# An mLSTM layer on Trainium2: decays put on the queries, the finish of its rows moved between its chunk steps

## What is computed

```python
log_d = jnp.where(tri, cum[..., :, None] - cum[..., None, :] + ig[..., None, :], NEG_INF)
inter = cum + m_st[..., None]
m_t = jnp.maximum(inter, jnp.max(log_d, axis=-1))
s_qk = jnp.einsum('bhctd,bhcsd->bhcts', q, k) * jnp.exp(log_d - m_t[..., None])
a_t = jnp.exp(inter - m_t)
num = (jnp.einsum('bhcts,bhcsv->bhctv', s_qk, v)
       + a_t[..., None] * jnp.einsum('bhcvk,bhctk->bhctv', c_st, q))
den = jnp.sum(s_qk, axis=-1) + a_t * jnp.einsum('bhck,bhctk->bhct', n_st, q)
out = num / jnp.maximum(jnp.abs(den), jnp.exp(-m_t))[..., None]
```

## Time and profile before

| | |
|---|---|
| median of 3 executions | 1573.1 us |
| lowest, highest | 1570.92, 1576.23 us |
| profiled execution, its own time | 1573.14 us |
| its span in the profile | 1571.3 us |
| outside the span (1573.14 less 1571.3) | 1.8 us |
| TensorE's granted clock over the span | 0.98 |
| TensorE busy | 1469.6 us, 94% |
| VectorE busy | 995.1 us, 63% |
| ScalarE busy | 755.6 us, 48% |
| GpSimd busy | 67.5 us, 4% |

### The profile page before, as it was taken

How to read it: one execution, slowest core, us unless ns; L and a number is a source line. 1 busy time by engine, 2 the same in 40 slices (tenths; PEclk the granted TensorE clock), 3 DMA queues, 4 the chain that set the end, 5 groups by cost and what they waited for, 6 DMA issues and landing times.

```text
span 1571.3 us, 24144 instructions
## 1 busy us (share of the span) xinstructions
PE 1469.6 (94%) x9392; PEld 1204.5 (77%) x9392; DVE 995.1 (63%) x2286; ACT 755.6 (48%) x1630; POOL 67.5 (4%) x76
## 2 busy tenths in 40 slices
PE   6999998999999999999979999798899899999998
PEld 4777756787777777888757777576687798789987
DVE  4647676564666548535674668576776567777753
ACT  4435576453655443231133546565566447555542
POOL 0000000100000100020000100001100120000000
PEclk9999999999999999999999999899999999999999
DMA  9131172322452322221461153514435542445553
GB/s 360 56 107 54 54 256 81 101 81 67 157 191 69 107 89 92 94 68 54 155 234 54 55 166 104 175 55 141 144 125 159 186 169 95 158 152 189 189 188 132
DMA packets 59866, 202.84 MB, mean 129 GB/s; under 512 B 7694, under 2 KB 10984, under 8 KB 59624
## 3 DMA queue, kind: packets, MB, share of 16 engines
q1 hardware_dynamic: 53568, 192.84, 35.6%
q10 hardware_dynamic: 6008, 7.40, 2.0%
q0 software_dynamic: 176, 1.06, 0.2%
HBM read 199.43 MB, written 1.84 MB: 128 GB/s over the span
## 4 chain that ended last, share of the span: by engine, by line
PE 71%; DVE 15%; ACT 5%; DMA 4%; issue 3%; POOL 1%; ACTq 0%; SPq 0%; DVEq 0%; POOLq 0%
PE ps L2216 65%; PE ps L2219 5%; DVE w_l L2886 2%; DVE st L2985 1%; DMA w_raw<-in_l_out 1%; DVE x L2894 1%; ACT w_h L2529 1%; DVE l_P L2890 1%; ACT l_P L2532 1%; DMA w_l_ada<-in_l_ada 1%; DVE m_P L3469 1%; DVE l_xn L2890 1%; DVE l_h_lat L2894 1%; POOL mstat L3563 1%; POOL pstat L3574 1%
## 5 line engine op out<-in xcount | busy, mean ns | idle before, releaser
L2886 DVE TENSOR_TENSOR w_l<-w_raw,w_h 128x1024 fp32r<-128x1024 f32 (+3 forms) x263 | 315.0, 1206 | 82.5 <-ACT w_h L2529 81.6
L2529 ACT ACTIVATE w_h<-w_raw 128x1024 fp32r<-128x1024 f32 (+3 forms) x263 | 271.1, 1042 | 111.9 <-DMA w_raw<-in_l_out 26.7
L2216 PE MATMUL ps<-w_h,l_hTh 128*128 128x512 f32 (+1 forms) x384 | 156.4, 407 | 0.3 <-DVE w_l L2886 0.2
L2216 PE MATMUL ps<-w_h,l_hTl 128*128 128x512 f32 (+1 forms) x384 | 152.1, 396 | 0.0
L2216 PE MATMUL ps<-w_l,l_hTh 128*128 128x512 f32 (+1 forms) x384 | 151.9, 396 | 0.0
L2532 ACT ACTIVATE l_P<-ps,st 128x512 f32<-128x512 f32 (+1 forms) x128 | 77.5, 606 | 84.7 <-DVE st L2894 59.2
L2216 PE MATMUL ps<-f_hTh,w_h 128*128 128x256 f32 x352 | 99.1, 281 | 0.0
L2216 PE MATMUL ps<-l_hTh,w_h 128*128 128x512 f32 (+1 forms) x264 | 98.5, 373 | 0.5 <-issue 0.5
L2216 PE MATMUL ps<-f_hTl,w_h 128*128 128x256 f32 x352 | 98.9, 281 | 0.0
L2216 PE MATMUL ps<-f_hTh,w_l 128*128 128x256 f32 x352 | 98.8, 281 | 0.0
L2216 PE MATMUL ps<-l_hTl,w_h 128*128 128x512 f32 (+1 forms) x264 | 97.7, 370 | 0.0
(11 more groups left out here) (444 smaller groups left out, 3475.7 us busy)
## 6 DMA issues: line engine op xcount, KB each, us to landing
w_raw<-in_l_ada SPq DMA_DIRECT2D x49, 512.0 KB, 4.6
w_raw<-in_l_z SPq DMA_DIRECT2D x32, 512.0 KB, 3.5
w_raw<-in_l_adg SPq DMA_DIRECT2D x32, 512.0 KB, 3.5
w_raw<-in_l_out SPq DMA_DIRECT2D x32, 512.0 KB, 4.5
w_raw<-in_m_merge SPq DMA_DIRECT2D x24, 512.0 KB, 3.2
w_raw<-in_f_gate SPq DMA_DIRECT2D x22, 512.0 KB, 3.3
w_raw<-in_f_up SPq DMA_DIRECT2D x22, 512.0 KB, 3.5
w_raw<-in_f_down SPq DMA_DIRECT2D x22, 512.0 KB, 4.3
```

The lines of the kernel that those rows point to most:

```text
L2216: return p.e.matmul(out, lhsT, rhs, start=start, stop=stop)
L2529: return p.e.activation(out, a, func, scale=scale)
L2886: return p.e.tensor_tensor(out, a, b, op)
```

## The change

- A query's state part is scaled before the matmul. The row `a` is halved and split in two parts (tiles `l_arl`, `l_arc`), four matmuls spread it over all partitions (`ml_scaled`, `l_ar*,l_pick`), and VectorE multiplies the queries by it (tile `l_qk`, or `l_k` in steps 4 and 5). The state's four matmuls, of 257 columns, then add to the same PSUM group as the local ones. The small matmuls, four operations of the denominator's chain, `ml_carried` and `ml_edge` are gone.
- The finish of a context tile is done tile by tile and sooner, and its transposes start before step 6; `fin_o`, squares and rows of latent tile 1 lie beside step 7.
- The gate row's 8 modulation blocks come first, with `ahead` 1 for 2.
- `split_to` at the end goes to out 3 rather than out 1. The rest of out 1 and out 3 is taken by GpSimd (`POOL_REST`), with a semaphore per slot.

```diff
+POOL_REST = {("l2_out", 1), ("l2_out", 3)}
...
-            weave(beside, upto(half, 8), 8, 14)
+            weave(beside, upto(half, 8), 8, 11)
...
-        mod = p.ada(PAIR, [(3, 0), (2, "gate"), (3, 1)], gate, ahead=2)
-        drain(braid(upto(steps, 6), upto(mod, 6), upto(ctx, 3)))
+        mod = p.ada(PAIR, [(2, "gate"), (3, 0), (3, 1)], gate, ahead=1)
+        weave(braid(upto(steps, 6), upto(mod, 6)), upto(ctx, 7), 7, 12)
         gate.free = p.fence()
-        drain(braid(steps, mod, ctx))
-        p.W.split_to(len(p.W.order) + 1, len(p.W.order) + 1)
+        weave(braid(upto(steps, 3), upto(mod, 3)), upto(ctx, 4), 4, 6)
+        lat = m.finish((1, 0), lambda: f, TRANS)
+        weave(braid(steps, mod), braid(upto(lat, 3), ctx), 6, 6)
+        p.W.split_to(len(p.W.order) + 3, len(p.W.order) + 3)
         f = p.fence()
-        lat = m.finish(LAT, f, TRANS)
...
+        def scaled(x):
+            d, c = steps[x]
+            b = p.take(pool)
+            p.ml_scaled(self, x, d, self.ORDER[d][c], b, self.qa(x))
+            p.give(b, ("lstm", "qa", x))
...
             if x < 6:
+                scaled(x + 2)
                 masked(nxt)
...
         for t in pair:
             p.fin_o(self, t, [self.htok[t, h] for h in range(4)])
             yield
-        for t in pair:
             p.fin_sq(self, t)
+            p.rows_rstd4(self, t)
             yield
-            p.rows_rstd4(self, t)
-        for t in pair:
             p.fin_rows(self, t)
             yield
...
+            y = p.mm(p.n.bank(bo[h], 257), m.Dt[x][:, h * 128:h * 128 + 128], m.va[:, t, h, :], True, c == 0)
+            if c == 0:
+                y.then_inc(*p.mark("lstm", "sum", x, h))
         for h in range(4) if c else ():
-            p.wait_ge(("lstm", "den", x))
-            p.mm(p.n.bank(bo[h])[:, 257:512], m.qk[:, h, t * 128:t * 128 + 128], m.C[:, 4 * d + h, 0:255], True, True).then_inc(
-                *p.mark("lstm", "carry", x, h))
+            p.wait_ge(("lstm", "qa", x), ("lstm", "C", x - 2, h))
+            p.mm(p.n.bank(bo[h], 257), m.qa(x)[:, h], m.C[:, 4 * d + h, :], False, True).then_inc(*p.mark("lstm", "sum", x, h))
+
+    def ml_scaled(p, m, x, d, t, b, out):
+        s0 = slice(t % 2 * 128, t % 2 * 128 + 128)
+        p.wait_ge(("gates", "ar"), p.B.freed[b])
+        for h in range(4):
+            pick = m.pick[:, 4 * d + h:4 * d + h + 1].to_broadcast([128, 128])
+            y = p.mm(p.n.bank(b)[:, h * 128:h * 128 + 128], pick, m.ar[t // 2][:, s0], True, True)
+        y.then_inc(*p.mark("lstm", "spread", x))
...
+    def ml_scaled(p, m, x, d, t, b, out):
+        four = p.n.bank(b).rearrange("p (h t) -> p h t", h=4)
+        p.wait_ge(("lstm", "spread", x), ("lstm", "qk", t), ("lstm", "state", x - 4, 3) if x in (4, 5) else None)
+        p.tt(out, m.qk[:, 0:4, t * 128:t * 128 + 128], four, ALU.mult).then_inc(*p.mark("lstm", "qa", x))
```

More of the change, by code:

```diff
@@ L953, in __init__ @@
         self.rounded = self.done = 0
+        self.rests = [0] * NR
     def next(self, name, i, ks, cols, raw=False, ahead=AHEAD):
@@ L959, in next @@
         b.nsplit = self.split_n
+        s = b.j % NR
         if not raw:
             self.split_n += 1
+            self.rests[s] += 1
+        b.rest, b.on_pool = (s, self.rests[s]), (name, i) in POOL_REST
         self.order.append(b)
-        s = b.j % NR
         view = lambda t: t[:, 0:ks * cols].rearrange("p (k n) -> p k n", k=ks)
         b.raw, b.h, b.l = view(n.w_raw[s]), view(n.w_h[s]), view(n.w_l[s])
-        b.ready = [("loaded", b.j)] if raw else [("w_rounded", b.nsplit), ("w_rest", b.nsplit)]
+        b.ready = [("loaded", b.j)] if raw else [("w_rounded", b.nsplit), ("w_rest", *b.rest)]
         self.p.w_load(b.j + NR)
@@ L1647, in chunks @@
         self.kE = lambda d, c: self.k0[d][:] if c == 0 else self.kt[:, self.ORDER[d][c], :]
+        rows = lambda t: self.qk[:, 0:4, t * 128:t * 128 + 128]
+        self.qa = lambda x: (self.k0[x - 4][:].rearrange("p (h t) -> p h t", h=4) if x in (4, 5) else
+                             rows(self.ORDER[steps[x][0]][steps[x][1]]))
         def exponents(x):
@@ L1671, in chunks @@
             bo = [p.take(pool) for _ in range(4)]
-            p.ml_local_mm(self, x, t, bo)
-            bd = p.take(pool) if c else None
-            p.ml_den(self, x, d, c, t, bo, bd, self.dn_tok.get((d, c - 1)))
-            if c:
-                p.give(bd, ("lstm", "last", x))
-            p.ml_carry_mm(self, x, d, c, t, bo)
-            dtok[x] = ("lstm", "carry" if c else "local", x, 3)
+            p.ml_local_mm(self, x, d, c, t, bo)
+            p.ml_den(self, x, d, t, bo, self.dn_tok.get((d, c - 1)))
+            dtok[x] = ("lstm", "sum", x, 3)
             yield
@@ L2686, in ml_max @@
         p.f(r["a"][:], r["a"][:], ACT.Exp).then_inc(*p.mark("gates", "a"))
+        p.wait_ge(("gates", "a"), p.stage_tok)
+        for x in range(2):
+            y = p.copy(m.ar[x][0:64], r["a"][:, 256 * x:256 * x + 256], scale=0.5)
+        y.then_inc(*p.mark("gates", "ah"))
         p.wait_ge(("gates", "nm_in"))
@@ L3151, in ml_max @@
         p.tt(m.negMr[64:128], m.negM[:], m.negMr[0:64].bitcast(F32), ALU.subtract).then_inc(*p.mark("gates", "M"))
+        p.wait_ge(("gates", "ah"))
+        for x in range(2):
+            y = p.stt(m.ar[x][64:128], r["a"][:, 256 * x:256 * x + 256], 0.5, m.ar[x][0:64].bitcast(F32), ALU.mult, ALU.subtract)
+        y.then_inc(*p.mark("gates", "ar"))
     def ml_cols(p, m, b, fence):
@@ L3200, in ml_masked, with ml_den @@
         p.tt(D[:], D[:], m.ST[:, t, :], ALU.mult).then_inc(*p.mark("lstm", "D", x))
[L3202 to L3205 removed]
+    def ml_scaled(p, m, x, d, t, b, out):
+        four = p.n.bank(b).rearrange("p (h t) -> p h t", h=4)
+        p.wait_ge(("lstm", "spread", x), ("lstm", "qk", t), ("lstm", "state", x - 4, 3) if x in (4, 5) else None)
+        p.tt(out, m.qk[:, 0:4, t * 128:t * 128 + 128], four, ALU.mult).then_inc(*p.mark("lstm", "qa", x))
+    def ml_den(p, m, x, d, t, bo, prev):
+        n, dn = p.n, m.dn[:, d]
+        p.wait_ge(("lstm", "sum", x, 3), prev)
         for h in range(4):
@@ L3219, in ml_den, with ml_local @@
         p.e.reciprocal(dn[:, 1], dn[:, 1]).then_inc(*p.mark("lstm", "recip", x))
-        if c:
-            p.wait_ge(("lstm", "recip", x))
-            p.stt(dn[:, 2], dn[:, 1], 0.5, a, ALU.mult, ALU.mult).then_inc(*p.mark("lstm", "gain", x))
-            p.wait_ge(("lstm", "gain", x))
-            p.tt(dn[:, 3], two[:, :, 0], dn[:, 2], ALU.mult).then_inc(*p.mark("lstm", "last", x))
-    def ml_local(p, m, x, d, c, t, h, b, fresh, old):
+    def ml_local(p, m, x, d, t, h, b, fresh, old):
         dst, src = m.h[t][:, h * 256:h * 256 + 256], p.n.bank(b, 256)
-        p.wait_ge(("lstm", "last" if c else "recip", x), ("lstm", "carry", x, h) if c else None)
+        p.wait_ge(("lstm", "recip", x))
         if fresh:
@@ L3566, in condition, with w_rest @@
         p.e.memset(p.n.phalf[:], -0.5).then_inc(*p.mark("begin", "half"))
+    def w_rest(p, b):
+        n, s, w = p.n, b.j % NR, b.words
+        if b.on_pool:
+            p.wait_ge(("w_rounded", b.nsplit))
+            out, raw, high = n.w_l[s][:, 0:w], n.w_raw[s][:, 0:w], n.w_h[s][:, 0:w].bitcast(F32)
+            p.e.tensor_tensor(out, raw, high, ALU.subtract).then_inc(n.sem(f"w_rest{s}"), 1)
     def rows_mean(p, rows, t):
```

71 lines of the change are left out of this document (21 added, 50 removed).

## The result

The changed kernel is **slower**: 1578.1 us (median of 20, 1573.0 to 1583.1) beside 1572.7 for the kernel before on the same chip, a ratio of 1.0037, 95% interval 1.0026 to 1.0049. Forecast was 1569.2, in a range of 1563.5 to 1574. A second set of executions gave 1.0041 (1.0027 to 1.0055).

What follows compares the result with a forecast made beforehand. TensorE (94% busy) was taken to wait for the late latent rows on VectorE's queue; 1573.1 less 5.3 gives 1567.8, with 2.4 for a GpSimd hold and queued power 1570.2, middle -3.9: 1569.2, range 1563.5 to 1574.

Steps and rivals of the forecast that it cites:

- stage -4.7: Modulation and out stage behind the z projection: the part of the forecast -3.9 beside the z projection's +0.8.
- the forecast's two cases: Whole kernel: 1567.8 us after a gain of 5.3, or 1570.2 with one VectorE hold and the queued power, 2.4.
- Two savings and four spreads fall into the z projection, where TensorE has no gap, +0.8: z projection: saves about 0.8 us per state group, pays 0.6 per spread of four matmuls; net +0.8.
- Rival 4: z projection: scaling doesn't pay; a scaled tile delaying a mask costs 0.7 in each of four steps, +3; no chance given.
- I cost them at nothing: Gates: two added roundings and two operations of 256 columns on VectorE, beside the query and key projection, cost nothing.
- the case that the cover is gone: Gates: if blocks were not split several ahead, the four added VectorE operations would cost 4 x 0.6 = 2.4 us.
- The state group and VectorE's operations: Chunk steps: four savings and two spreads behind the z projection, TensorE -2.0; VectorE net -2.0 in each of six steps.
- The order followed step by step: Steps 4 to 7: queues followed with these prices; new 1.9 us wait at 790.3, step 7's sum at 805.5, 3.2 later.
- Projection at 816.6, latent transposes at 822.8: Stage's end: projection at 816.5 to 816.7 against 817.5, first latent transposes at 822.8 rather than 829.5; gain 5.3 us.
- ScalarE's old stop is gone with this: Modulation stage: gate row's blocks first puts `l_gth` ahead of any rounding, ending TensorE's stop from 806.4 to 811.1.
- rival 3: Context's projection: more TensorE gaps keep the clock at its lower level, net +3 to +5.5, 1576 to 1578.6; chance 0.07.
- I carry no gain from it: Stage: the halved clock remains, as TensorE still stands some 4 us ahead of 816.7 and 3 ahead of 822.8.

Runs made afterwards that it cites:

- old-order kernels: Changed kernel with bank, rests and decay-row edits, modulation-stage order as in the kernel before: 0.9988, again 0.9978 of the kernel before; with the bank edit undone, 1.0033.
- The new order alone: Kernel before with only the new lines of the modulation stage, `finish` and the out projection's `weave`, keeping its own sums: 1.0010 of the kernel before.

## Why the prediction was wrong, point by point

Forecast -3.9 as the sum of: gates 0, z projection +0.8, stage -4.7. Measured in the profiles: +1.5, +7.0, -1.55, together +6.9, where the medians differ by 5.4. (The middle of the forecast's two cases, 1567.8 and 1570.2, is 1569.0; the 1569.2 on record is 0.2 off.)

- **"Two savings and four spreads fall into the z projection, where TensorE has no gap, +0.8".** The step that failed: it prices the spreads as work and puts their wait at nothing. As work even the 0.8 was too much: without the stops the stretch takes 61.5, no more than before (61.56), and a spread takes 0.5 rather than 0.6. What I left out is whom the spread waits for. I had it, for the steps behind ("a spread that itself waits for the bank of ScalarE's weights"), and did not ask it of steps 0 to 3, where ScalarE's queue holds `l_z` ahead of those weights. Rival 4 looked at the right place with the wrong mechanism, a mask that is late, at +3. Price, by the runs: 3.4 or 3.5 of standing in all five profiles that have the bank order, and behind it 3.4 of clock in two of them and 0 in three; the stretch is 4.0 or 7.1 longer than where that bank is given back behind the state's.
- **Gates, "I cost them at nothing".** 1.5 in the profile; the 1.7 of low clock that some profiles add is not theirs, since it comes without the wait too. The cover was ample in blocks, but VectorE's queue is in order: a wait of 1.05 for ScalarE ahead of a rest is a wait for that rest. The 2.4 named for the case that the cover is gone held as a bound, but it was priced as work, and the loss was a wait.
- **The state group and VectorE's operations.** Right in kind and a little short in size: TensorE's work in the stage fell by 2.8 (85.3 to 82.5, the stage less standing and clock), where I had 2.0. By the profiles of the old-order kernels this alone makes the stage 2.4 to 3.2 shorter.
- **The order followed step by step.** Shifted by the 7.3 by which step 4's sum is later, the forecast gives 790.0 for step 5's sum (789.70), a stop for the context rows of 1.9 that ends at 799.5 (1.71, 799.35), 803.8 for step 6's (803.41) and 812.8 for step 7's (813.68, after a stop of 1.31 for `l_G` that I did not have). The method held.
- **Projection at 816.6, latent transposes at 822.8.** Shifted, 823.9 and 830.1; measured 829.06 and 836.02. That is 15.4 and 22.3 behind step 7's sum, where 10 to 12 and 17 to 20 were named. Some 0.9 comes from step 7 and 4.0 from the two holds by GpSimd; 0.3 is left at the projection and 1.0 at the transposes, not followed further. I had bounded the holds at 0 to 3.4 and taken the middle between no hold and a case of 2.4 (one hold and the queued power); there are two, and each is 2, not 1.7. The rule that stood beside this term, and that I gave half weight, held at both rests: the Trainium skill, "SBUF — State Buffer", section "Who interferes with whom", has the second to issue block fully, and here VectorE, coming second, waited until GpSimd's rest was through.
- **"ScalarE's old stop is gone with this", and the gain with it.** The stop went and the gain did not come. The new order alone has a longer stage (107.8, one profile, mostly clock); the old order under the new sums has a shorter one (101.0 to 101.7 in three) than before (104.1). TensorE's standing in the stage was 14.2 to 17.7 in all fourteen profiles, whichever stop was taken away: the forecast put the -4.7 down to the wrong half of the change.
- **The clock, rival 3 (0.07).** Its place was wrong. At the latent stage the clock cost less than before (2.5, 4.6); in the z projection it cost 3.4 in both profiles of this kernel, behind stops that I had not foreseen. "I carry no gain from it" was fair, no loss was not.

## What to carry to other kernels

When a change adds a small matmul group to a dense stretch, look up which bank it takes and who gave that bank back last: a pool that hands out the longest-free bank can hang it on an engine that has nothing to do with it. Give banks back in the order in which their readers finish, not in the order in which the code is written; here one line is worth 4 to 7 us. And before an order is credited with a gain, run the order alone and the operations alone, and look where each edit puts the work of every queue: in this stage each stop that was taken away came back elsewhere, in three kernels partly because the edit had put the transposes ahead of matmuls that were ready.
